# Attention's softmax a pair at a time beside the projections, its bias added in PSUM, and later adaLN units, in a four-layer diffusion step

## The reference

```
def na_context(h, wqkv, wo):
    qkv = (h @ wqkv).reshape(B, N, 3, N_HEADS, HEAD_DIM)
    s = einsum('bqhd,bkhd->bhqk', q, k) * ATTN_SCALE
    p = softmax(s)
    return (p @ v) @ wo, k, v
def na_latent(h, ctx_k, ctx_v, wqkv, wo, rpb):
    s_loc = q @ kg * ATTN_SCALE + bias      # -inf outside the column window
    s_ctx = q @ ctx_k * ATTN_SCALE
    p = softmax(concatenate([s_loc, s_ctx]))
    return (p_loc @ vg + p_ctx @ ctx_v) @ wo
```

## Time and profile before

| | us |
|---|---|
| median of 3 runs | 1415.18 (1412.69 to 1416.93) |
| the profiled execution | 1411.53 |
| its span | 1409.7 |
| PE busy | 1292.4 (92%) |
| DVE busy, ACT busy | 387.2 (27%), 329.5 (23%) |
| chain that ended last | PE 76%, DMA 15%, DVE 6%, ACT 2%, issue 2% |
| moved by DMA | 535.19 MB, 380 GB/s in the mean |

### The profile page before, as it was taken

The page is one execution under the profiler, slowest core; times in us unless marked ns, Lnnn a source line. Parts: engine busy times, 40 slices in busy tenths (PEclk is TensorE's granted clock), DMA queues, the critical chain, the costliest instruction groups (busy, mean ns, idle before and its releaser), DMA issues.

```text
span 1409.7 us, 18775 instructions
## 1 busy us (share of the span) xinstructions
PE 1292.4 (92%) x6817; PEld 605.6 (43%) x6817; DVE 387.2 (27%) x825; ACT 329.5 (23%) x674; POOL 38.8 (3%) x76
## 2 busy tenths in 40 slices
PE   3879999997998879999999899999999869999996
PEld 1334434342783434544434364444434345444342
DVE  1341222313111432331222312322231343322224
ACT  1222212212101222321212222212222252222122
POOL 3010000000100010000000000000000000000000
PEclk9899999999999889999999999999999989999998
DMA  9999999999974895899999997799999995999995
GB/s 375 420 418 420 421 421 421 422 421 422 337 290 162 349 408 204 316 416 421 421 421 422 421 394 283 295 423 421 421 421 422 420 387 204 420 421 422 421 422 236
DMA packets 87257, 535.19 MB, mean 380 GB/s; under 512 B 11192, under 2 KB 13336, under 8 KB 25760
## 3 DMA queue, kind: packets, MB, share of 16 engines
q1 hardware_dynamic: 82336, 527.47, 91.6%
q0 software_dynamic: 3120, 5.23, 1.2%
q10 hardware_dynamic: 1744, 1.73, 0.4%
HBM read 532.26 MB, written 2.12 MB: 379 GB/s over the span
## 4 chain that ended last, share of the span: by engine, by line
PE 76%; DMA 15%; DVE 6%; ACT 2%; issue 2%; SPq 0%; DVEq 0%; ACTq 0%
PE ps L1597 28%; PE ps L1646 12%; DMA ring<-in_moe_w_up_dram 7%; PE ps L1582 5%; PE ps L1209 4%; PE ps L1307 4%; PE ps L1333 4%; DMA ring<-in_ada_w_dram 3%; PE ps L1658 3%; PE ps L1346 2%; DMA ring<-in_pool_w_dram 2%; PE ps L1620 2%; DMA ring<-in_attn_wqkv_dram 2%; PE ps L1631 2%; PE ps L1613 1%
## 5 line engine op out<-in xcount | busy, mean ns | idle before, releaser
L1597 PE MATMUL ps<-ring,xg 128*64 128x512 f32 x1024 | 466.9, 599 | 8.7 <-DMA ring<-in_moe_w_up_dram 8.7
L1599 PE MATMUL ps<-ring,xg 128*64 128x512 f32 x1024 | 467.2, 599 | 0.0
L1597 PEld LDWEIGHTS ps<-ring,xg 128*64 128x64 f32 x1024 | 132.2, 137 | 265.4 <-issue 257.6
L1646 PE MATMUL ps<-ring,act 128*64 128x512 f32 x1024 | 231.5, 593 | 6.2 <-DVE act L1138 6.1
L1147 DVE SCALAR_TENSOR_TENSOR gb<-ps,gslot,g2x 128x512 f32<-128x512 f32 x128 | 90.2, 747 | 356.2 <-PE ps L1646 356.2
L1646 PEld LDWEIGHTS ps<-ring,act 128*64 128x64 f32 x1024 | 76.0, 137 | 146.3 <-issue 131.2
L1599 PEld LDWEIGHTS ps<-ring,xg 128*64 128x64 f32 x1024 | 132.3, 137 | 0.0
L1209 PE MATMUL ps<-ring,cact 128*32 128x512 f32 x768 | 101.1, 660 | 31.9 <-DMA ring<-in_ada_w_dram 15.2
L726 ACT ACTIVATE y_hi<-gb 128x512 fp32r<-128x512 f32 x128 | 77.2, 627 | 196.2 <-DVE gb L1147 117.9
L713 ACT ACTIVATE gu<-ps 128x512 f32<-128x512 f32 x64 | 38.2, 597 | 225.3 <-PE ps L1599 225.3
L1156 DVE TENSOR_TENSOR y_lo<-gb,y_hi 128x512 fp32r<-128x512 f32 x128 | 84.6, 691 | 17.6 <-ACT y_hi L726 16.4
(11 more groups left out here) (190 smaller groups left out, 1078.5 us busy)
## 6 DMA issues: line engine op xcount, KB each, us to landing
ring<-in_moe_w_gate_dram SPq DMA_DIRECT2D x128, 1024.0 KB, 16.9
ring<-in_moe_w_up_dram SPq DMA_DIRECT2D x128, 1024.0 KB, 18.4
ring<-in_moe_w_down_dram SPq DMA_DIRECT2D x128, 1024.0 KB, 18.5
ring<-in_ada_w_dram SPq DMA_DIRECT2D x96, 1024.0 KB, 17.2
ring<-in_attn_wqkv_dram SPq DMA_DIRECT2D x12, 1024.0 KB, 19.1
ring<-in_attn_wo_dram SPq DMA_DIRECT2D x4, 1024.0 KB, 9.3
ring<-in_fourier_w_dram SPq DMA_DIRECT2D x4, 1024.0 KB, 24.2
ring<-in_pool_w_dram SPq DMA_DIRECT2D x2, 1024.0 KB, 27.3
```

What stands on the lines that cost most here:

```text
L1597: mg = pe.matmul(ps[0:SLOTS, B_GU, :], xg[:, b, e, :], wg[:, i * F:(i + 1) * F], start=(b == 0), stop=(b == DB - 1))
L1599: mu = pe.matmul(ps[SLOTS:P, B_GU, :], xg[:, b, e, :], wu[:, i * F:(i + 1) * F], start=(b == 0), stop=(b == DB - 1))
L1646: mm = pe.matmul(ps[r * SLOTS:(r + 1) * SLOTS, B_Y, :], act[:, j, :], w[:, i * D + r * HALF:i * D + (r + 1) * HALF], start=(j == 0), stop= ...
```

## The change

Attention's work is cut into halves. The order of units becomes: half of table 4, column blocks 0 (q) and 2 (k), the rest of table 4, block 4 (v), table 5, blocks 1 and 3, table 6, block 5, table 7, half of the output matrix, half of table 8, the other half, the rest. Pairs 0 to 3 need only blocks 0, 2 and 4, so pair 0's scores stand right after the flips and turns, and from there PE has a projection job, adaLN units, or both between a pair's scores and its turn. `scale_bias_max` becomes `bias_max`: the scores stay in PSUM, DVE takes a maximum there, adds the bias (now divided by the scale) onto the bank, takes the other maximum, and `exps` on ACT reads the bank, with the scale as its factor, and writes `soft`. There is one pair of score banks (6 and 7), so the next scores wait for the exponentials of the last. `bias` lies in `gb`, and pairs 0 to 3 are stored in `o_first`, since hT is still read. `FILLS` takes 1, 2 and 1 units for layers 1 and 3, and 1, 2 and 0 for layer 2; the other units stand inside the mixer. In layer 3 the pool unit comes before the second half of table 11, whose DVE row comes behind the pool additions, and the second gate rows behind that.

```
 BEFORE_EXPERTS = [
...
-    ada_units(4) + [u for c in range(6) for u in matrix_units("qkv", c)]
-    + ada_units(5) + ada_units(6) + ada_units(7) + ada_units(8)[:4]
-    + matrix_units("wo", 0) + matrix_units("wo", 1) + ada_units(8)[4:],
+    ada_units(4)[:4] + matrix_units("qkv", 0) + matrix_units("qkv", 2) + ada_units(4)[4:]
+    + matrix_units("qkv", 4) + ada_units(5) + matrix_units("qkv", 1) + matrix_units("qkv", 3) + ada_units(6)
+    + matrix_units("qkv", 5) + ada_units(7) + matrix_units("wo", 0) + ada_units(8)[:4] + matrix_units("wo", 1) + ada_units(8)[4:],
...
-    ada_units(11) + [("pool", 1, 0)],
+    ada_units(11)[:4] + [("pool", 1, 0)] + ada_units(11)[4:],
...
-FILLS = {1: (4, [0, 2, 6, 8]), 2: (9, [0, 2, 5, 5]), 3: (11, [0, 2, 6, 8])}
+FILLS = {1: (4, [0, 1, 3, 4]), 2: (9, [0, 1, 3, 3]), 3: (11, [0, 1, 3, 4])}
...
-                def scale_bias_max(hp):
+                def bias_max(hp):
...
-                    v.tensor_scalar(soft[:, par, :, 0:P], banks[:, :, 0:P], SCALE, None, ALU.mult)
-                    v.tensor_scalar(soft[:, par, :, 2 * P:3 * P], banks[:, :, 2 * P:3 * P], SCALE, None, ALU.mult)
-                    link(v.scalar_tensor_tensor(soft[:, par, :, P:2 * P], banks[:, :, P:2 * P], SCALE,
-                                                bias[:, 2 * hp:2 * hp + 2, :], ALU.mult, ALU.add))
-                    v.tensor_reduce(mstat[:, par, 0, 0:4:2], soft[:, par, :, 0:P], AX_X, ALU.max)
-                    link(v.tensor_reduce(mstat[:, par, 0, 1:4:2], soft[:, par, :, P:3 * P], AX_X, ALU.max))
+                    banks = ps[:, 6:8, 0:3 * P]
+                    v.tensor_reduce(mstat[:, par, 0, 0:4:2], banks[:, :, 0:P], AX_X, ALU.max)
+                    link(v.tensor_tensor(banks[:, :, P:2 * P], banks[:, :, P:2 * P], bias[:, 2 * hp:2 * hp + 2, :], ALU.add))
+                    link(v.tensor_reduce(mstat[:, par, 0, 1:4:2], banks[:, :, P:3 * P], AX_X, ALU.max))
...
                 def scores(hp):
-                    if hp >= 2:
-                        pe.wait_ge(s_max, hp - 1)
+                    if hp >= 1:
+                        pe.wait_ge(s_exp, 4 * hp)
...
+                attend(0)
+                w, wk = weights(1), weights(3)
+                by_channel(Q1A, w, 0)
+
+                ada_turn(5)
+                turn(2)
+                scores(3)
+                attend(1)
+                by_channel(K1A, wk, 0)
...
+                scores(7)
+                ada_turn(6)
+                by_token(V1B, w, 1)
+                ada(7, 0, 2, l, base)
+                emptied(V1A)
+                emptied(V1B)
+                attend(4)
+                turn(6)
+                attend(5)
+                ada(7, 2, 4, l, base)
+                turn(7)
+                attend(6)
+                ada(7, 4, ADA_UNITS, l, base)
+                attend(7)
                 gates(l, 0)
+                ada_turn(7)
...
-                        gates(l, 0)
+                        first_gates(l, 0)
                         pool_tokens(l)
-                        gates(l, 1)
+                        first_gates(l, 1)
+                        ada(11, 4, ADA_UNITS, l, base)
+                        second_gates(l, 0)
+                        second_gates(l, 1)
                         ada_turn(11)
                         normed(2 * l + 1)
```

More of the change, by code:

```diff
@@ new lines, in attention @@
+                bias_max(4)
+                copy_output(2)
+                normalise(4)
+                bias_max(5)
+                copy_output(3)
+                normalise(5)
+                empty(K1B, blocks(kT, 6, 2))
+                bias_max(6)
+                ada_rows(6, l, base)
+                normalise(6)
+                bias_max(7)
+                ada_mods(6)
+                normalise(7)
+                empty(V1B, vtok[:, 1, 512:1024])
+                for hp in range(4, PAIRS):
+                    copy_output(hp)
@@ L1344, in by_token, with done, weights, by_channel @@
+                def done(i, mm):
+                    if i in CLOSES:
+                        mm.then_inc(s_used, 2)
+                    else:
+                        mm.then_inc(s_job, 1)
+                def weights(cc):
+                    return [unit(UNIT_AT[("qkv", cc, h)], l, base) for h in range(2)]
+                def by_channel(i, w, n):
+                    room(i)
+                    for d in range(2):
                         for b in range(DB):
-                            at = (b % 4) * 512
@@ L1389, in scores @@
                             part = slice(e * HD, (e + 1) * HD)
[L1390 removed]
+                            mm = pe.matmul(ps[:, 6 + e, i * P:(i + 1) * P], q[part], keys[part], start=True, stop=True)
                     mm.then_inc(s_sc, 1)
@@ new lines, in attention @@
+                w = weights(0)
+                by_channel(Q0, w, 0)
+                by_channel(Q0 + 1, w, 1)
+                w = weights(2)
+                by_channel(K0, w, 0)
+                by_channel(K0 + 1, w, 1)
+                pe.wait_ge(s_ck, 48)
+                pe.wait_ge(s_bias, 16 * 6)
+                flat = braw[:, :, :].rearrange("p h k -> p (h k)")
+                for b in range(4):
+                    room(FLIPS + b)
+                    mm = pe.matmul(ps[:, JOB_BANK[FLIPS + b], :], kattn[:, 1, :], flat[:, b * 512:(b + 1) * 512], start=True, stop=True)
+                    done(FLIPS + b, mm)
@@ new lines, in attention @@
+                attend(1)
+                by_channel(K1A, wk, 0)
+                turn(3)
+                emptied(Q1A)
+                emptied(K1A)
+                scores(4)
+                attend(2)
+                by_channel(Q1B, w, 1)
+                turn(4)
+                scores(5)
+                attend(3)
+                by_channel(K1B, wk, 1)
+                ada(6, 0, 4, l, base)
+                turn(5)
+                emptied(Q1B)
+                emptied(K1B)
+                scores(6)
@@ new lines, in attention @@
+                ada(6, 4, ADA_UNITS, l, base)
+                w = weights(5)
+                by_token(V1A, w, 0)
+                turned(K_TURN1, [kT[:, 4 + i, 0:SEQ] for i in range(4)])
+                scores(7)
[8 more added lines that the diff above has]
+                ada(7, 2, 4, l, base)
```

297 lines of the change are left out of this document (140 added, 157 removed).

## The result

The changed kernel took 1372.8 us (median of four, 1371.5 to 1376.8), the kernel before beside it 1414.1 (four, 1412.7 to 1416.9): a ratio of 0.969, 95% interval 0.967 to 0.971. Forecast were 1377.0 us, in a range of 1369 to 1394. The profiled execution is the slowest of the four (1376.75 us); its span is 34.8 us shorter than that of before, 1374.9 for 1409.7, where 38.2 were forecast. A second profile of the same kernel has 1372.4 (37.3 shorter).

A forecast was written before the change was run, and what follows sets the result against it. Not DMA-bound throughout: attention was a DVE and ACT chain with too little PE work beside it. 31.6 for attention, 0.3 and 6.3 make 38.2 us; 1411.5 becomes 1373.3, plus 3.7 for the median 1377.0, range 1369 to 1394.

The forecast's parts named there:

- The first job: Ahead of layer 1's attention: first projection at 352.0 instead of 361.47, 9.5 us gained, 3.6 given back for four adaLN units.
- The stops of 20.3 us: Layer 1's attention: PE's waits for DVE behind the first job, 20.3 us, go except 2 us of small stops.
- DVE's removed scalings: Attention: two scalings of 0.42 us per pair, 6.7 in all, worth nothing beyond the stops taken away.
- Half clock, 7.4 us: Layer 1's attention: time lost to slow adaLN pieces (4.8), turns (1.3), scores and attends (about 1.3) comes back.
- The chain: One attention pair on DVE and ACT: 4.8 us, some 5.5 with handovers, fits beneath PE's work; turn(0) has 6.9 + 0.6.
- Rival 5: Attention: one pair of score banks makes the chain serial; at 13 us a pair 54 us slower, 1431; 3 in 100.
- Operations on PSUM: DVE in attention: no dearer from PSUM by the rows; by the skill's cycle table 1.5 us more over eight pairs.
- Rivals 1 and 2: Attention: PE still stops at pairs, 14 us, 1391, 15 in 100; half clock without stops, 15 us, 1392, 5 in 100.
- Layer 2, 0.3 us gained: First Fourier stage begins 2 us earlier, but the next adaLN piece still waits and has five units, not three: 0.3 us.
- Layer 3, 6.3 us: Earlier transposes and pool bring the second norm's transposes 6.3 us forward, with 0.6 taken for half clock.
- The experts: Layer 1's experts start with a full ring as before; what follows is shifted, not changed, and groups keep their pace.
- rival 4: Layer 1's experts start with the ring short, 2.49 us per missing unit, up to 30 us, 1407 or above; 3 in 100.

The follow-up runs named there:

- fill1_back: Changed kernel with layer 1's adaLN units as before (two, four and two ahead of attention, none of table 4 inside): 1383.5 us, 9.2 more than the changed kernel beside it.
- bias_in_sbuf: Changed kernel's order, but DVE scales and adds the bias into SBUF and reduces there, ACT working in place: 1372.4 us, ratio to before 0.967.
- chain_7: Changed kernel with the 512-column maximum repeated seven times more in each pair: 1382.1 us (1381.4 to 1384.5).
- chain_3: Changed kernel with the 512-column maximum repeated three times more in each pair: 1371.7 us (1370.7 to 1373.4).
- layer3_back: Changed kernel with layer 3 as before (pool unit behind all of table 11, gate rows and DVE's row in old order): 1379.9 us, 5.6 more.
- old_order_mods_first: Kernel before, with DVE's adaLN table store ahead of normalising the next pair in pairs 2, 4 and 6: 1407.2 us beside 1418.7, ratio 0.992.

## Why the prediction held, step by step

- **The first job**: 352.0 forecast, 352.37 and 353.43 measured. The gain of 9.5 was 9.1 and 8.0 in the two profiles; less the 3.6 us of units, 5.5 and 4.4. `fill1_back` puts the whole step at 6.0 to 8.3 by profiles, since its stop for weights is followed by half clock, and at 9.2 by times. Shown, with its size uncertain upwards. The prediction didn't ask what clock the first projection gets behind that stop.
- **The stops of 20.3 us**, of which 2.0 were kept: they went, and 0.7 us are left. Two parts are shown apart: 9.0 us of it (and 2.5 of half clock) was an order of lines on DVE, worth 11.5 us alone; the PSUM softmax was worth at most about 3 in the old order and 0 in the new one. The rest, the turns and attends above all, is put down to the interleaving as what is left over; no run has the interleaving alone. DVE's removed scalings were costed at nothing behind that, and `bias_in_sbuf` shows it.
- **Half clock, 7.4 us**: all of it came back in the first profile, where the stage lasts 175.4 us and 174.6 and 2.0 were written: that term was too careful by 1.2 us. Eight of the eleven profiles with the new order have 175.4; in the second one of the changed kernel the first projection began at half clock, and the stage lasts 176.9 (the other two are `fill1_back`, with four units fewer, and `chain_7`).
- **The chain**: forecast 4.8 us, 5.5 with handovers; measured 4.8 with them (pairs 2 and 6: 6.5 and 5.5). Turn(0) was named as the one with least cover, 7.5 against 5.5; it was 7.3 against 4.8, so it had 2.57 us, and by `chain_3` and `chain_7` this is what decides. Rival 5, the serial chain, would have had to be 12.5 us long to take back all the gain; at 9.8 us the loss was 8 to 10 us.
- **Operations on PSUM**: DVE's maximum of 512 columns took 0.691 us from PSUM, 0.676 from SBUF, that of 256 columns 0.425 and 0.420; ACT's exponentials of 256 columns were faster, 0.471 for 0.493. The Trainium skill, VectorE: DVE Perf Modes, "Rules for kernel authors", advises a copy to SBUF ahead of several operations. With it (`bias_in_sbuf`) the time was the same. The measured differences are 15 and 5 ns; the 62 cycles of that page's cycle table (section "The TRN2 errata — SBUF-src ops pay a fixed extra latency per instruction") at its 0.96 GHz would be an estimated 65 ns. The chain without the copy is 0.8 us shorter.
- **Rivals 1 and 2**, stops at the pairs or half clock among them without one: neither came. The Trainium skill, TensorE: Matmul & The Clock Gate, "HAM oscillation — how this bites in real kernels", describes bursts between waits that start slow each time. `chain_7` made such waits of 1.8 to 2.0 us: behind two the small matmuls ran slow, behind one at full clock. Behind the stop of 2.45 us ahead of the Fourier stage four of seven profiles ran slow. So a wait of about 2 us was followed by half clock in six cases of ten here, and was not sure to be; behind the stop of 4.09 us in layer 3 it was in seven of seven.
- **Layer 2, 0.3 us gained**: right in the mean by luck. I had let the first Fourier stage "begin 2 us earlier" for two units removed, and had two units more behind it take most of that back. From the last 16 expert matmuls it began at 14.73 us before and at 11.95 now, 2.8 earlier; the stop of 1.04 us behind it stayed, and the two units cost 1.7. With the clock full the second stage is then 1.1 us earlier than before (24.56 for 25.65); with half clock behind the stop of 2.45 us it is 0.4 to 0.6 later (26.07 to 26.25). Three of seven profiles have the one, four the other, which is 0.15 us gained in the mean. The step asked what waits next at the stage's start, but not what clock it gets there.
- **Layer 3, 6.3 us**: 5.6 by the times of `layer3_back`. From the last 16 expert matmuls of layer 2 to the second norm's transposes there are 47.25 us before, 42.03 and 41.84 now: 5.2 and 5.4 earlier, and with their slow stretch the first expert matmul of layer 3 is 6.0 and 7.1 earlier. That these transposes came 33.6 us earlier in the first profile and not 38 is mostly the lead with which the layer began, 28.4 instead of 31.9, and that lead has lost 4.7 us to the three chance stretches named above. The half clock that I took at 0.6 was more, 1.8 on the gate rows and 1.1 on turn and transposes in the first profile. These do belong to the order of work: the stop of 4.09 us ahead of the gate rows, and half clock behind it, is in all seven profiles that have this layer.
- **The experts**: rival 4 didn't come; layer 1's first expert matmul (545.32 us) doesn't wait for a load, and their groups take the same 599 ns a matmul.
- **The sum**: 38.2 forecast for the profiled execution, 34.8 and 37.3 measured in two profiles, and 41 between the medians beside each other (44 in the second set). By stages, 31.6 forecast for the first job and attention are 33.4 and 31.1, 0.3 for layer 2 up to its experts are -2.0 and 1.1, and 6.3 for layer 3 are 6.0 and 7.1; what lies between lost 2.7 and 2.0, where nothing was forecast. The forecast time of 1377.0 is 4 above the median. That the medians of the kernel before lie 3 to 7 us above its profiled time in every set isn't explained by these profiles. One candidate is the load ahead of the first projection, 3.14 us of stop in its profile and 8.12 in that of `old_order_mods_first`; the changed kernel has no such stop. Another is the clock: its executions of 1415 us and more have 0.964 to 0.971, the profiled one 0.972. No run separates them.

## What to carry to other kernels

Read cover as a time on the waiting engine: from the end of the chain on the other engines to the instruction that reads it. Here a chain 2.2 us longer used up all but 0.4 of 2.57 us and cost nothing, one 5.1 us longer stopped PE at the three pairs with 3 us or less, and the cover told beforehand that keeping the scores in PSUM would bring nothing. Before a large reordering, look at the order on the engine that is waited for: two lines moved on DVE gave a quarter of the gain. When a unit of work is taken out ahead of a norm, name the stop that opens there, and price the slow matmuls behind it with it. And before a difference of 1 or 2 us is put down to an edit, look for the same place in a second profile of the same kernel: three stretches that looked like losses of the new order were missing there.

## What the runs showed of the hardware

The granted clock in these traces is full or half, and half follows stops that look short: 1.8 us at pair 0 in `chain_7`, 2.45 before the Fourier stage. It is partly chance: the Fourier stage was slow in four profiles of seven, and the same program had its first experts' gathers of layer 1 slow in one execution (1.42 us for two matmuls that took 0.58 in the other). Other places come again: both profiles of the changed kernel have slow expert pieces at 322 us, behind a wait of 2.14 us for a load in the first and 2.11 in the second:

```profile
320.91 0.61 PE L1693 MATMUL ps<-ring,xg 128*64 128x512 f32 x1 [2.14 <-DMA ring<-in_moe_w_up_dram]
...
322.36 1.06 PE L1693 MATMUL ps<-ring,xg 128*64 128x512 f32 x1
...
325.63 0.59 PE L1693 MATMUL ps<-ring,xg 128*64 128x512 f32 x1
```

Some 3 us of work run slow there, at a cost of about 1.5 us. A few such spells more or less would be enough for the 5 us by which the nine times of the changed kernel differ, and the granted clocks of these executions fit (0.985 for the fastest, 0.976 for the slowest), though they don't prove the cause; with that scatter differences of 2 us between variants stay open here. The surprise was that work for nothing is cheaper than a stop: some 17 idle matmuls made the kernel 2.5 to 4.8 us faster, by which kernel it is compared with. For how long a filler has to run, and behind which stops it isn't needed, no run here says.
